# Decode stage of a two-layer hybrid trunk: one common step list replaced by a list for each engine

## The chip, the cores and the metric

The kernel runs on one core of a Trainium2 chip. The metric is device time in microseconds of one execution, the median of the runs. A core has TensorE (matrix products, here in fp32), VectorE, ScalarE, GpSimd and SyncE, which issues the DMAs; each works through its own instruction stream in order, and they wait for each other with counting semaphores.

## The reference, cut to what matters

One inference step through two layers. Each layer projects the input once and feeds three groups; the stage that is changed computes two of them side by side: the cached attention of eight decode rows, and the state recurrence of the 1024-token prompt.

```python
def mla_decode_attention(q_nope, q_pe, ckv, kpe, w_uk, w_uv, ckv_pool, kpe_pool, page_table):
    ckv_past = ckv_pool[page_table].reshape(B, -1, KV_LORA)      # 8 x 4096 x 256
    kpe_past = kpe_pool[page_table].reshape(B, -1, MLA_ROPE)     # 8 x 4096 x 64
    q_abs = jnp.einsum('blhd,rhd->blhr', q_nope, w_uk)
    s_past = (einsum(q_abs, ckv_past) + einsum(q_pe, kpe_past)) * ATTN_SCALE
    ...
    p = softmax(concatenate([s_past, s_new]))
    o_lat = einsum(p[..., :P], ckv_past) + einsum(p[..., P:], ckv)
    return einsum('blhr,rhd->blhd', o_lat, w_uv)

def rwkv7_time_mix(...):
    def step(S, inp):
        r_t, k_t, v_t, kk_t, b_t, d_t = inp
        sa = einsum('bhvk,bhk->bhv', S, kk_t)
        S = S * d_t[:, :, None, :] - sa[..., None] * b_t[:, :, None, :] + v_t[..., None] * k_t[:, :, None, :]
        return S, einsum('bhvk,bhk->bhv', S, r_t)
```

## The kernel before, in words

A layer is a sequence of blocks: the modulation, the projections with the prompt's attention, the decode stage, and the output projection. All engines meet between blocks. The decode stage (lines 1404 to 1860) does two things in one stream.

**Decode attention.** The 256 pages of a layer's cache are handled in 16 halves h of 16 pages (128 tokens each), two halves per decode row. SyncE fetches a half with two calls of `load` (lines 399 to 404), a quad q of eight pages of 160 KB each, page numbers read from the page table. The quads lie in a ring of six (QS = 6), so of three halves. For q from 6 on SyncE first waits for `pg_free`, which TensorE raises when PV has read the quad that lay there:

```python
for q in range(4, 2 * NH):
    if q >= QS:
        sp.wait_ge(pg_free, q - QS + 1)
    load(sp, q)
```

Ahead of quad 4 the same queue issues a few small transfers for the sample rows' state, and behind quad 5 eight small ones. Quads 0 to 3 are loaded before or at the start of the stage.

The steps of a half, with their lines:
- turn (L1748, VectorE): transposes one block of 32 rows in 128 x 512 elements, ten per half, n = 10 h + rb, into a ring of four buffers. The first of a half (rb = 0) waits for both quads (`pg_in`); each waits until TensorE has used the block four before it.
- S (L1589, TensorE): scores of one turned block, 16 matmuls in the trace per S (8 in the program). Ten per half.
- MX (L1808 to L1815, VectorE): the maximum; EX (L1690, ScalarE): the exponentials.
- PT (L1598, TensorE; L1700, ScalarE): transposes the probabilities.
- PV (L1607, TensorE): probabilities times pages, 32 matmuls in the trace; half-way and at its end it raises `pg_free`.

**State recurrence.** The prompt is handled in 8 pairs p of two chunks of 64 tokens; one pair goes with two halves, 2p and 2p+1. `prepare(p, n)` builds a pair's matrices: MA (L1467; VectorE L1764 to L1773, `levels` L1756), five levels of an inverse in which X (L1515; last L1494) goes from TensorE to a copy on ScalarE (L1664) and Y (L1522; last L1501, L1503) from TensorE to VectorE (L1781, L1783), then AK (L1474, L1777), TA and TB (L1480, L1482, L1487; ScalarE L1649, L1656). `follow(p, n)` carries the state through the pair before: Z (L1538, L1541; ScalarE L1670), U (L1549; L1674), H (L1556, L1558; VectorE L1791, then the scaled state `Sg`, L1795), OO (L1565 to L1569; L1677).

**What sets the order.** One list `plan` is walked by TensorE, VectorE and ScalarE alike; each does its part of a step or nothing. Per half it runs S S | two steps | S S | PT | two steps | S S | PV | two steps | S S | two steps | S S | step | MX | step | EX | step. PT and PV are those of the half before. Where the list says S of block n, VectorE makes the turn of block n + 2. After the last pair a tail does the last PT, PV, the last chain and the combination FC.

Of the kernel before, what the change touches and what calls it, by code (L numbers as in the profile page):

```python
# [26 lines left out]
S = 1024  # L27
NS = 8
T = S + NS
# [70 lines left out]
def bass_hybrid_trunk(nc, a):  # L100
    with ExitStack() as ctx:
# [92 lines left out]
        with nc.Fori(0, DEPTH) as layer:  # L194
# [345 lines left out]
            with nc.Block() as block:  # L540
# [517 lines left out]
                def _(dve):  # L1058
# [229 lines left out]
                    for what, n, x in plan:  # L1288
# [114 lines left out]

            STEPS = ["MA", "Z0", "X1", "U0", "Y1", "H0", "X2", "Z1", "Y2", "U1", "X3", "H1", "Y3", "OO",
                     "X4", "AK", "Y4", "TA", "X5", "TB", "Y5"]
            chain = ("Z", "U", "H", "O")


            plan = []
            for h in range(NH):  # L1410
                mine = [("rw", n) for n in (STEPS[0:11] if h % 2 == 0 else STEPS[11:])]
                for rb in range(0, NB, 2):
                    plan += [(h, "S", rb), (h, "S", rb + 1)]
                    if rb == 2 and h:
                        plan.append((h - 1, "PT", 0))
                    if rb == 4 and h:
                        plan.append((h - 1, "PV", 0))
                    if rb < 8:
                        plan += [(h // 2, *mine.pop(0)), (h // 2, *mine.pop(0))]
                rest = [(h // 2, *x) for x in mine]  # L1420
                plan += rest[:1] + [(h, "MX", 0)] + rest[1:2] + [(h, "EX", 0)] + rest[2:]
            plan += [(NH - 1, "PT", 0), (NS, "rw", "Z0"), (NH - 1, "PV", 0), (0, "FC", 1), (NS, "rw", "U0"), (0, "FC", 2), (NS, "rw", "H0"),
                     (0, "FC", 3), (NS, "rw", "Z1"), (0, "FC", 4), (NS, "rw", "U1"), (0, "FC", 5), (NS, "rw", "H1"), (0, "FC", 6),
                     (NS, "rw", "OO")]

            with nc.Block() as block:
# [25 lines left out]
                def _(pe):  # L1452
# [119 lines left out]

                    for h, what, g in plan:
                        if what == "rw" and g[0] in chain:
# [58 lines left out]
                def _(act):  # L1633
# [44 lines left out]

                    for h, what, g in plan:
                        if what == "rw" and g[0] in chain:  # L1680
# [57 lines left out]
                def _(dve):  # L1738
# [20 lines left out]
                    def prepare(p, n):  # L1759
                        k = p % 2  # L1760
                        B = PB[:, 5, :].rearrange("p (v d c) -> p v d c", v=2, d=4)
                        if n == "MA":
# [9 lines left out]
                            dve.drain()  # L1772
                            dve.transpose(Tm.rearrange("p d c -> p (d c)"), Tc.rearrange("p d c -> p (d c)")).then_inc(tm_done, 1)  # L1773
                            levels(2, LEVELS).then_inc(bm_done, 1)
                        elif n == "AK":
# [9 lines left out]
                    def follow(p, n):  # L1785
                        B = PB[:, 6, 0:P].rearrange("p (f v) -> p f v", f=2)
                        if n[0] == "H":
                            i = 2 * p + int(n[1])
                            dve.wait_ge(hh_full, i + 1)
                            for f in range(2):  # L1790
                                op = dve.scalar_tensor_tensor(S0[:, (i + 1) % 4, f, :], B[:, f, :], ecol[:, f, i:i + 1], Sg[:, f, :], ALU.mult, ALU.add)  # L1791
                            op.then_inc(st_done, 1)
                            if i + 1 < NCH:
                                dve.drain()
                                dve.tensor_tensor(Sg, S0[:, (i + 1) % 4], ecol[:, :, i + 1:i + 2].broadcast_to([P, 2, 64]), ALU.mult)  # L1795

                    for h, what, g in plan:
                        if what == "rw" and g[0] in chain:
                            if h >= 1:
                                follow(h - 1, g)  # L1800
                        elif what == "rw":
                            prepare(h, g)
                        elif what == "S":
                            if NB * h + g + 2 < NB * NH:
                                turn(NB * h + g + 2)
                        elif what == "MX":
# [377 lines left out]
```

## Time and profile before

| | us |
|---|---|
| median of 3 runs | 2041.21 |
| lowest and highest | 2038.88, 2041.49 |
| the profiled execution: its time | 2037.07 |
| the profiled execution: its span | 2035.4 |
| decode stage, layer 0 | 625 to 880 |
| decode stage, layer 1 | 1635 to 1893 |
| TensorE, VectorE, ScalarE busy | 1865.2, 895.6, 494.7 |

All times below are microseconds from the start of the profiled span. An engine's busy time leaves out semaphore waits and the issue of DMAs; a matmul's end is modelled. Waits are put down to the instruction that ended them. SPq is SyncE's DMA issue: a row "x16" there is 16 fetches issued one behind the other.

### The profile page before, as it was taken

The numbers are of one execution on the slowest core, as the hardware profiler recorded it, in microseconds if no ns is written. First come the engines' busy times: TensorE is split into PE (matmuls) and PEld (weight loads), VectorE is DVE, ScalarE is ACT, GpSimd is POOL, SyncE is SP. The second block draws the span as 40 slices with busy tenths as digits, with TensorE's granted clock in tenths as the row PEclk, the third lists the DMA queues.
The fourth block names the chain that finished last, engine by engine and source line by source line (L and its number), as shares of the span: only waits on it lengthen the run. The fifth ranks groups of instructions, "written<-read, shape, count | busy, mean of one in ns | idle before, by whom it ended". The sixth has DMA issues, their size and how long they took to land. (4 is left out here: it accounts for less than half of the span.)

```text
span 2035.4 us, 45818 instructions
## 1 busy us (share of the span) xinstructions
PE 1865.2 (92%) x19360; PEld 1164.3 (57%) x19360; DVE 895.6 (44%) x1984; ACT 494.7 (24%) x1164; POOL 172.6 (8%) x158
## 2 busy tenths in 40 slices
PE   4899999999987999899949999999999879998898
PEld 2565676666654666654326656766666546665543
DVE  2024134222766676654230340332318577775542
ACT  3111012222412333311131110222224123333201
POOL 0010000011334000000000100000212240000000
PEclk9899999999999999979989999999999899999899
DMA  9500000000205666341075001010001166562411
GB/s 388 207 11 27 21 21 32 21 21 13 59 26 159 185 188 180 109 178 42 32 301 213 0 27 32 11 32 22 21 22 50 28 186 186 176 186 83 178 42 42
DMA packets 103927, 191.18 MB, mean 94 GB/s; under 512 B 17162, under 2 KB 87260, under 8 KB 100004
## 3 DMA queue, kind: packets, MB, share of 16 engines
q1 hardware_dynamic: 103716, 188.19, 27.9%
q8 instruction: 154, 2.52, 0.5%
q14 instruction: 57, 0.47, 0.1%
HBM read 175.41 MB, written 21.19 MB: 97 GB/s over the span
## 5 line engine op out<-in xcount | busy, mean ns | idle before, releaser
L771 PE MATMUL PB<-RB,R 128*128 128x344 f32 x1632 | 496.1, 457 | 0.0
L771 PEld LDWEIGHTS PB<-RB,R 128*128 128x128 f32 x1632 | 303.7, 191 | 159.6 <-issue 19.7
L1946 PE MATMUL PB<-RB,R 128*128 128x512 f32 x512 | 221.2, 593 | 0.0
L1589 PE MATMUL PB<-WUQ,Q 32*32 32x256 f32 x5120 | 191.0, 385 | 14.7 <-DVE WUQ L1748 9.4
L1748 DVE STREAM_TRANSPOSE WUQ<-RB 128x512 f32<-128x512 f32 x316 | 197.0, 676 | 5.5 <-DMA RB<-in_cache 5.3
L1946 PEld LDWEIGHTS PB<-RB,R 128*128 128x128 f32 x512 | 97.0, 190 | 120.8 <-issue 118.6
L931 ACT ACTIVATE R<-PB 128x344 f32<-128x344 f32 x90 | 41.2, 457 | 423.4 <-PE PB L771 423.4
L1184 DVE TENSOR_TENSOR PB<-PB,CST 128x128 f32<-128x128 f32 x64 | 18.8, 294 | 226.3 <-PE PB L791 226.3
L1589 PEld LDWEIGHTS PB<-WUQ,Q 32*32 32x32 f32 x5120 | 90.0, 104 | 46.0 <-DVE WUQ L1748 23.1
L619 PE MATMUL PB<-RB,R 128*128 128x344 f32 x288 | 88.5, 472 | 10.8 <-PEq L225 10.8
L619 PEld LDWEIGHTS PB<-RB,R 128*128 128x128 f32 x288 | 57.1, 199 | 41.4 <-issue 14.8
L246 PE MATMUL PB<-R,WUQ 128*32 128x512 f32 x192 | 33.5, 667 | 49.2 <-DMA R<-in_w_ada 49.2
L1066 DVE COPY R<-PB 128x320 f32<-128x320 f32 x16 | 7.9, 491 | 149.7 <-PE PB L630 149.7
L788 PE MATMUL PB<-RB 128*128 128x128 f32 (+2 forms) x192 | 71.5, 495 | 0.0
L630 PE MATMUL PB<-RB 128*128 128x320 f32 x256 | 69.2, 432 | 0.0
L1607 PE MATMUL PB<-RB 128*32 128x256 f32 x1024 | 67.4, 404 | 1.9 <-ACT RB L1700 1.9
L2041 POOL TENSOR_TENSOR sm<-sm,small 128x1 f32<-128x1 f32 (+1 forms) x18 | 9.9, 550 | 698.6 <-DVE sm L2073 698.6
L942 ACT ACTIVATE R<-PB,sm,small 128x128 f32<-128x128 f32 (+3 forms) x64 | 53.2, 832 | 56.8 <-DVE sm L1188 56.2
L760 PE MATMUL PB<-R,RB 128*128 128x256 f32 x256 | 61.1, 383 | 0.0
L630 PEld LDWEIGHTS PB<-RB 128*128 128x128 f32 x256 | 48.6, 190 | 20.3
L1700 ACT ACTIVATE RB<-PB 64x256 f32<-64x256 f32 x128 | 48.3, 378 | 39.1 <-PE PB L1598 37.8
L2015 ACT ACTIVATE RB<-PB 128x1024 f32<-128x1024 f32 x16 | 16.3, 1021 | 161.2 <-PE PB L1946 161.2
(355 smaller groups left out, 2619.6 us busy)
## 6 DMA issues: line engine op xcount, KB each, us to landing
RB<-in_cache SPq DMA_DIRECT2D x512, 160.0 KB, 2.6
R<-in_w_ada SPq DMA_DIRECT2D x16, 1536.0 KB, 17.4
R<-in_w_in SPq DMA_DIRECT2D x44, 512.0 KB, 3.7
RB<-in_w_out SPq DMA_DIRECT2D x8, 1024.0 KB, 9.9
RB<-out_x_stream SPq DMA_DIRECT2D x2, 4096.0 KB
out_x_stream<-RB SPq DMA_DIRECT2D x16, 512.0 KB
RB<-in_x_prompt SPq DMA_DIRECT2D x1, 4096.0 KB
RB<-in_w_kv SPq DMA_DIRECT2D x2, 1280.0 KB, 5.6
```

The lines of the kernel that those rows point to most:

```text
L619: mm = pe.matmul(bigbank(n)[:, c, :], ring[:, i % 4, k, :], hT[:, k, c * CH:(c + 1) * CH], start=(k == 0), stop=(k == KT - 1))
L630: mm = pe.matmul(smlbank("kv", t)[:, 0:KVW], hT[:, k, cols(t)], wkv_in[:, k, :], start=(k == 0), stop=(k == KT - 1))
L760: mm = pe.matmul(jobbank(j)[:, 0:256].rearrange("p (w c) -> p w c", w=2), hT[:, k, cols(c)], w2, start=(k == 0), stop=(k == KT - 1))
L771: mm = pe.matmul(jobbank(j)[:, 0:CH], ring[:, blkno[n] % 4, k, :], hT[:, k, chunk(c)], start=(k == 0), stop=(k == KT - 1))
L788: pe.matmul(sbank(2 * u + e)[:, c:c + w], qT[:, h, i * P:(i + 1) * P], kT[:, h, c:c + w], start=True, stop=False)
L931: act.activation(to, jobbank(j)[:, 0:CH], fn).then_inc(pj_free[j % 2], 1)
L942: act.activation(pbuf(n), sbank(n), ACT.Exp, bias=nbr[:, n:n + 1], scale=scq[:, i:i + 1], accum_out=Lr[:, n:n + 1]).then_inc(ex_done, 1)
L1589: mm = pe.matmul(PB[qp[o], 2 * (h % 2) + q % 2, 0:256], Q4[qp[q], g, :], k[qp[q], c], start=(g == 0), stop=(g == NB - 1), skip_group_check ...
L1607: mm = pe.matmul(PB[qp[c], 7, f * KVL:(f + 1) * KVL], PT[:, s, 32 * c:32 * c + 32], qpage(q)[:, (4 * s + c) % 8, RP:RP + KVL], start=(h == ...
L1700: op = act.activation(PT[hp[w], :, e * 64:(e + 1) * 64], t4[hp[e], :, w, :], ACT.Identity)
L1748: op = dve.transpose(KTr[:, n % 4], pages[:, :, fcol(rb):fcol(rb) + 32])
L1946: mm = pe.matmul(PB[0:n, 2 * (t % 2) + hf, :], mixT[:, k, cols(t)], wo[:, k, hf * 512:(hf + 1) * 512], start=(k == 0), stop=(k == 5))
```

## The change

The common list `plan` goes. TensorE, VectorE and ScalarE get a list each for one pair, in words; `pair_plan` writes it out for p = 0 to 7 and appends the same tail. In a word, S or T and two digits are score or turn: the half of the pair and the block (T20 and T21 are the first two turns of the next pair). PT, PV, MX and EX carry 0 or 1 for the pair's halves, and - for the second half of the pair before. So turns stand singly in VectorE's list, and no longer two ahead of the same S.

Two steps are cut off from others on VectorE. LV is `levels(2, LEVELS)`, which was the end of MA. G is the scaled state `Sg`, which followed H at once, behind a drain; now it has its own place, and drains only in the tail. The computation, the buffers, the semaphores' meanings, SyncE's queue and GpSimd's work stay as they are.

```diff
-            plan = []
-            for h in range(NH):
-                mine = [("rw", n) for n in (STEPS[0:11] if h % 2 == 0 else STEPS[11:])]
...
+            PE_PAIR = (
+                "S00 Z0 MA S01 S02 S03 U0 S04 PT- H0 X1 S05 Y1 Z1 S06 U1 X2 S07 H1 S08 S09 S10 Y2 PV- X3 OO Y3 S11 AK "
+                "S12 X4 PT0 S13 TA Y4 S14 S15 S16 S17 S18 TB S19 X5 PV0 Y5"
+            ).split()
+            DVE_PAIR = (
+                "T02 T03 T04 MA T05 H0 T06 LV Y1 G0 T07 T08 T09 T10 T11 T12 Y2 H1 T13 MX0 G1 Y3 T14 AK T15 T16 T17 "
+                "T18 T19 Y4 T20 T21 MX1"
+            ).split()
+            ACT_PAIR = (
+                "Z0 U0 MA X1 Z1 U1 X2 PT- X3 OO EX0 X4 PT0 TA TB X5 Y5 EX1"
+            ).split()
...
+                        elif n == "LV":
                             levels(2, LEVELS).then_inc(bm_done, 1)
...
                             op.then_inc(st_done, 1)
+                        elif n[0] == "G":
+                            i = 2 * p + int(n[1])
                             if i + 1 < NCH:
-                                dve.drain()
+                                if p == NS - 1:
+                                    dve.drain()
                                 dve.tensor_tensor(Sg, S0[:, (i + 1) % 4], ecol[:, :, i + 1:i + 2].broadcast_to([P, 2, 64]), ALU.mult)
+                                if p == NS - 1:
+                                    dve.drain()
...
-                        elif what == "S":
-                            if NB * h + g + 2 < NB * NH:
-                                turn(NB * h + g + 2)
+                        elif what == "T":
+                            turn(NB * h + g)
```

**TensorE, where a PV stands.** Before, in the first half of pair 1, from the second S pair to PV (L1607). L1589 is S (x16 in the order is two S), L1598 PT, L1515 an X, L1549 U, L1522 a Y.

```order
L1589 MATMUL PB<-WUQ,Q 32x256 x16
L1598 MATMUL PB<-CST,grow 128x128 x4
L1515 MATMUL PB<-RB 32x32 x16
L1549 MATMUL PB<-RB,R 64x64 x4
L1589 MATMUL PB<-WUQ,Q 32x256 x16
L1607 MATMUL PB<-RB 32x256 x16
L1522 MATMUL PB<-RB 32x32 x16
```

Now, in the same pair: from U1 (L1557) and X2 (L1523) to the first PV (L1615). L1597 is S (x8 is one), L1564 and L1566 are H1, L1530 is Y2.

```order
L1557 MATMUL PB<-RB,R 64x64 x4
L1523 MATMUL PB<-RB 32x32 x16
L1597 MATMUL PB<-WUQ,Q 32x256 x8
L1564 MATMUL PB<-R 64x64 x2
L1566 MATMUL PB<-WUQ,R 64x64 x2
L1564 MATMUL PB<-R 64x64 x2
L1566 MATMUL PB<-WUQ,R 64x64 x2
L1597 MATMUL PB<-WUQ,Q 32x256 x24
L1530 MATMUL PB<-RB 32x32 x16
L1615 MATMUL PB<-RB 32x256 x16
```

PV of the half before stood behind the sixth S of its half's successor; now PV- stands behind the eleventh S of the pair, and the chain's H0, Z1, U1 and H1 are ahead of it.

**TensorE, the other PV of a pair.** Before, in the second half: X4, two S, PV, AK (L1474).

```order
L1515 MATMUL PB<-RB 32x32 x16
L1589 MATMUL PB<-WUQ,Q 32x256 x16
L1607 MATMUL PB<-RB 32x256 x16
L1474 MATMUL PB<-RB,R 64x128 x8
L1522 MATMUL PB<-RB 32x32 x16
```

Now, at the end of the pair: Y4, five S, TB (L1495), S19, X5 (L1502), PV0.

```order
L1530 MATMUL PB<-RB 32x32 x16
L1597 MATMUL PB<-WUQ,Q 32x256 x40
L1495 MATMUL PB<-CST,R 128x128 x2
L1597 MATMUL PB<-WUQ,Q 32x256 x8
L1502 MATMUL PB<-RB 32x32 x8
L1615 MATMUL PB<-RB 32x256 x16
```

It moved from behind the pair's sixteenth S to behind its twentieth, and AK, TA and TB now stand ahead of it.

**VectorE, the turns in the second half's beginning.** Before, from MX (L1808) through two turns (L1748), H1 with its scaled state (L1791, L1795) and Y3 to four turns.

```order
L1815 TENSOR_SCALAR sm<-sm,CST 128x1
L1748 STREAM_TRANSPOSE WUQ<-RB 128x512 x2
L1791 SCALAR_TENSOR_TENSOR R<-PB,ecol,RB 128x64 x2
L1795 TENSOR_TENSOR RB<-R,ecol 128x128
L1781 TENSOR_TENSOR RB<-RB,PB 128x128
L1783 STREAM_TRANSPOSE RB<-RB 128x128
L1748 STREAM_TRANSPOSE WUQ<-RB 128x512 x4
```

Now, from G0 (L1807) through the turns T07 to T12 (L1756), Y2 and H1 (L1800) to T13 and MX0.

```order
L1807 TENSOR_TENSOR RB<-R,ecol 128x128
L1756 STREAM_TRANSPOSE WUQ<-RB 128x512 x6
L1790 TENSOR_TENSOR RB<-RB,PB 128x128
L1792 STREAM_TRANSPOSE RB<-RB 128x128
L1800 SCALAR_TENSOR_TENSOR R<-PB,ecol,RB 128x64 x2
L1756 STREAM_TRANSPOSE WUQ<-RB 128x512
L1821 TENSOR_REDUCE sm<-PB 128x1
```

T10, the first turn of the second half and the one that waits for that half's pages, now stands fourth in a row of six turns, ahead of Y2, H1 and MX0.

## Rows read from the trace of the kernel before

**Rows 1.** The page: busy us (share of the span) x instructions, by engine.
```profile
PE 1865.2 (92%) x19360; PEld 1164.3 (57%) x19360; DVE 895.6 (44%) x1984; ACT 494.7 (24%) x1164; POOL 172.6 (8%) x158
```
**Rows 2.** Windows, pairs 2 to 6: us, PE, PEld, DVE, ACT, POOL busy, PEclk, DMA, GB/s.
```profile
684.55:831.50 146.95, 135.37 (x4334) 91.97 (x4325) 105.95 (x261) 54.11 (x171) 0.00 (x0) 1.00 0.61 182
1696.30:1843.80 147.50, 136.15 (x4336) 92.06 (x4326) 105.94 (x261) 54.12 (x171) 0.00 (x0) 1.00 0.61 182
```
**Rows 3.** TensorE's waits, 686 to 833: waiter <- releaser: total us, times, longest.
```profile
PE PB L1467 <- ACT R L1661: 2.2, 5, 0.4
...
PE PB L1515 <- DVE RB L1773: 2.0, 5, 0.4
...
PE PB L1589 <- DVE WUQ L1748: 1.1, 5, 0.2
```
**Rows 4.** SyncE's fetches: timeline (start, us, xcount); issue to landing; waits, 680 to 880.
```profile
653.12 10.92 SPq L404 DMA_DIRECT2D RB<-in_cache  x16
...
664.95 10.76 SPq L404 DMA_DIRECT2D RB<-in_cache  x16
...
679.29 10.39 SPq L404 DMA_DIRECT2D RB<-in_cache  x16
...
723.20 12.59 SPq L404 DMA_DIRECT2D RB<-in_cache  x16
...
752.16 12.02 SPq L404 DMA_DIRECT2D RB<-in_cache  x16
...
1663.41 10.52 SPq L404 DMA_DIRECT2D RB<-in_cache  x16
...
1675.38 11.95 SPq L404 DMA_DIRECT2D RB<-in_cache  x16
...
1838.52 11.71 SPq L404 DMA_DIRECT2D RB<-in_cache  x16
...
DMA to landing us min/median/max: 2.0/2.6/4.1
...
SPq L401 <- PE PB L1607: 25.0, 10, 3.5
```
**Rows 5.** Timeline: first turn and score of pair 1, and the tail's PT.
```profile
650.46 1.30 DVE L1748 STREAM_TRANSPOSE WUQ<-RB 128x512 f32<-128x512 f32 x2 [2.20 <-DMA RB<-in_cache]
...
651.32 0.45 PE L1589 MATMUL PB<-WUQ,Q 32*32 32x256 f32 x8 [1.17 <-DVE WUQ L1748]
...
862.96 0.66 PE L1598 MATMUL PB<-CST,grow 128*128 128x128 f32 x4 [2.08 <-ACT grow L1690]
```
**Rows 6.** Timeline of pair 4, layer 0, from S00; TensorE, then VectorE's maximum.
```profile
742.81 0.37 PE L1589 MATMUL PB<-WUQ,Q 32*32 32x256 f32 x1
...
750.26 1.93 PE L1607 MATMUL PB<-RB 128*32 128x256 f32 x32
752.12 0.45 PE L1522 MATMUL PB<-RB 32*32 32x32 f32 x32
...
757.30 0.45 PE L1515 MATMUL PB<-RB 32*32 32x32 f32 x32 [0.42 <-DVE RB L1783]
...
767.79 1.15 PE L1589 MATMUL PB<-WUQ,Q 32*32 32x256 f32 x32
768.87 0.44 PE L1480 MATMUL PB<-CST,RB 128*128 128x128 f32 x2
...
771.77 0.37 PE L1589 MATMUL PB<-WUQ,Q 32*32 32x256 f32 x1
...
757.17 0.65 DVE L1808 TENSOR_REDUCE sm<-PB 128x1 f32<-128x512 f32 x1
...
758.65 1.29 DVE L1748 STREAM_TRANSPOSE WUQ<-RB 128x512 f32<-128x512 f32 x2
```
**Rows 7.** Windows around a lower granted clock (PEclk), layer 1; columns as in rows 2.
```profile
1659.50:1670.90 11.40, 5.50 (x163) 3.31 (x148) 9.49 (x18) 5.02 (x17) 10.84 (x6) 1.00 0.51 147
1670.90:1674.30 3.40, 3.37 (x48) 1.41 (x52) 1.75 (x3) 0.00 (x0) 1.22 (x4) 0.51 0.77 238
```

More of the change, by code:

```diff
@@ L1402, in bass_hybrid_trunk @@
             fcol = lambda rb: RP + 32 * rb if rb < 8 else 32 * (rb - 8)
-            STEPS = ["MA", "Z0", "X1", "U0", "Y1", "H0", "X2", "Z1", "Y2", "U1", "X3", "H1", "Y3", "OO",
-                     "X4", "AK", "Y4", "TA", "X5", "TB", "Y5"]
-            chain = ("Z", "U", "H", "O")
-            plan = []
-            for h in range(NH):
-                mine = [("rw", n) for n in (STEPS[0:11] if h % 2 == 0 else STEPS[11:])]
[L1412 to L1421, printed above, removed]
@@ L1422, in bass_hybrid_trunk @@
-            plan += [(NH - 1, "PT", 0), (NS, "rw", "Z0"), (NH - 1, "PV", 0), (0, "FC", 1), (NS, "rw", "U0"), (0, "FC", 2), (NS, "rw", "H0"),
-                     (0, "FC", 3), (NS, "rw", "Z1"), (0, "FC", 4), (NS, "rw", "U1"), (0, "FC", 5), (NS, "rw", "H1"), (0, "FC", 6),
-                     (NS, "rw", "OO")]
+            chain = ("Z", "U", "H", "G", "O")
+            PE_PAIR = (
+                "S00 Z0 MA S01 S02 S03 U0 S04 PT- H0 X1 S05 Y1 Z1 S06 U1 X2 S07 H1 S08 S09 S10 Y2 PV- X3 OO Y3 S11 AK "
+                "S12 X4 PT0 S13 TA Y4 S14 S15 S16 S17 S18 TB S19 X5 PV0 Y5"
+            ).split()
@@ new lines, in bass_hybrid_trunk, with pair_plan @@
+            DVE_PAIR = (
[5 more added lines that the diff above has]
+            ).split()
+            def pair_plan(words):
+                out = []
+                for p in range(NS):
+                    for w in words:
+                        if w[0] in "ST" and w[1] in "012":
+                            out.append((2 * p + int(w[1]), w[0], int(w[2])))
+                        elif w[:2] in ("PT", "PV", "MX", "EX"):
+                            out.append((2 * p - 1 if w[2] == "-" else 2 * p + int(w[2]), w[:2], 0))
+                        else:
+                            out.append((p, "rw", w))
+                return [x for x in out if 0 <= x[0] < NH] + TAIL
@@ L1426, in bass_hybrid_trunk @@
+            TAIL = [(NH - 1, "PT", 0), (NS, "rw", "Z0"), (NH - 1, "PV", 0), (0, "FC", 1), (NS, "rw", "U0"), (0, "FC", 2), (NS, "rw", "H0"),
+                    (NS, "rw", "G0"), (0, "FC", 3), (NS, "rw", "Z1"), (0, "FC", 4), (NS, "rw", "U1"), (0, "FC", 5), (NS, "rw", "H1"),
+                    (0, "FC", 6), (NS, "rw", "OO")]
             with nc.Block() as block:
@@ L1571, in follow @@
                             mm.then_inc(oo_full, 1)
-                    for h, what, g in plan:
+                    for h, what, g in pair_plan(PE_PAIR):
                         if what == "rw" and g[0] in chain:
@@ L1677, in follow @@
                             act.activation(A3[:, :, p * P:(p + 1) * P], PB[:, 6, 0:2 * P].rearrange("p (f t) -> p f t", f=2), ACT.Identity).then_inc(oo_done, 1)
-                    for h, what, g in plan:
+                    for h, what, g in pair_plan(ACT_PAIR):
                         if what == "rw" and g[0] in chain:
@@ L1792, in follow @@
                             op.then_inc(st_done, 1)
+                        elif n[0] == "G":
+                            i = 2 * p + int(n[1])
                             if i + 1 < NCH:
-                                dve.drain()
+                                if p == NS - 1:
+                                    dve.drain()
                                 dve.tensor_tensor(Sg, S0[:, (i + 1) % 4], ecol[:, :, i + 1:i + 2].broadcast_to([P, 2, 64]), ALU.mult)
-                    for h, what, g in plan:
+                                if p == NS - 1:
+                                    dve.drain()
+                    for h, what, g in pair_plan(DVE_PAIR):
                         if what == "rw" and g[0] in chain:
```

## The prediction, made before the result

> **What bounds the kernel now.** Read the page first: TensorE is busy for 92% of the span, VectorE for 44% [rows 1]. So only what moves TensorE's work, or the waits in it, can move the end. The change touches one stage, the decode stage, which runs once in each of two layers (625 to 880 us and 1635 to 1893 us). Its eight pairs p = 0 to 7 repeat one pattern; I call the start of a pair's first score step S00, and of the first step of its second half S10.
>
> Second, the windows over pairs 2 to 6 [rows 2]: 146.95 and 147.5 us for five pairs, so **a pair takes 29.4 and 29.5 us**, of which TensorE is busy 27.1 and 27.2 and VectorE 21.2. Third, TensorE's waits in that stretch [rows 3]: many of 0.2 to 0.7 us each, on VectorE and ScalarE in turn; with the smaller rows of that answer they make 2.3 us per pair. These are the waits that own lists can take away. Were they all to go, the pair would take 27.1 us. VectorE, at 21.2 us busy, could follow.
>
> Fourth, and this decides my forecast, the queue that fetches the pages. A half needs 16 pages; they go into a ring of three halves, and SyncE may fetch those of half h only when the PV step of half h-3 has read the old ones. In that queue a half's 16 fetches take 10.4 to 12.6 us [rows 4]; the 22 halves from the one at 679.29 to the one at 1838.52 that were fetched apart have a mean of 11.3. Landing comes 2.6 us (median) after a fetch's issue. Today SyncE still waits for PV, 25.0 us in ten halves of layer 0 [rows 4], so the queue has some 2.5 us to spare per half, and VectorE waits for pages only once per layer, at pair 1, by 2.2 us in layer 0 [rows 5].
>
> **The way from a PV to the scores that need its ring place.** Step by step: PV starts at 750.26, the first fetch at 752.16 [rows 4, 6]: 1.9 us. 16 fetches: 11.3. Last issue's end to landing: 2.6 less its own 0.33, 2.27. Turning the first block, to the score on it: 650.46 to 651.32 [rows 5], 0.86. Sum **16.3 us** (15.4 to 17.6 with the shortest and longest fetches). Today PV starts 7.45 us after S00 (742.81 to 750.26) and the S00 that needs its pages comes at 771.77, 21.5 us after that PV [rows 6]: 5 us of slack.
>
> **The change part by part.**
>
> *PV moves back.* In the new TensorE list PV- stands behind eleven S steps instead of six, and behind H0, Y1, Z1, U1, X2, H1 and Y2 as well. The cost in front of it: 7.45, less the 1.1 us of waits in it (2.2, 2.0 and 1.1 us in five pairs, ahead of MA, X1 and the third pair of S [rows 3]), plus five S at 0.54 (32 matmuls, two S, are started in 1.08, 767.79 to 768.87) 2.7, plus Y1 to U1 without their four S, 752.12 to 756.88, 4.76 - 2.16 = 2.6, plus H1, which I put at 0.8, twice the mean of those six steps [rows 6]: 12.4 us after S00. PV0 comes at the pair's end, behind S19 and X5. With a pair of 27.1 us the first leaves 14.7 us until the next S00, and PV0 (two S, Y2, and what follows up to X5: about 12.8 us after S10) leaves 27.1 - 12.8 = 14.3 until the next S10. Both are under 16.3. **So the waits on VectorE and ScalarE go, and a wait for pages takes their place.**
>
> The new period follows from two loops. First: S00, 12.4 us to PV-, 16.3 to the next S00; I add 0.5 because VectorE, which stood at T20, has then two turns of 0.6, the maximum (1.5) and T02 to T04 to do, which makes S03, S05 and S07 some 0.2 us late each [rows 6]. Sum 29.2. Second, since SyncE fetches in order: S10, 1.0 us to PV-, 1.9 to the first fetch, both halves' fetches 23.3 (10.92 + 10.76, and 10.52 + 11.95, back to back, with what lies between [rows 4]), and 3.1 to the score: 29.3. Both say **29.2 us per pair**, against 29.4 and 29.5: 5 x 0.2 + 5 x 0.3 = 2.5 us gained in both layers. Bounds: fetches of 10.4 or 12.6 in every half give 28.3 and 30.5; means over ten halves will lie closer, 28.5 to 29.9, or -7 to +7 us in all against the 29.2.
>
> *Start of the stage.* Pair 1 starts when quads 4 and 5 have landed, at 651.32 in layer 0 [rows 5]; layer 1 has the same wait. Their fetches stand behind small transfers, not behind a PV, so what pair 0 gains is lost again: nothing. Pair 1's S10 needs the next half, whose fetches end at 664.04 and 1673.93 whatever TensorE does [rows 4]: S10 at 667.2 and 1677.1. PV- is 1.0 later, the first fetch 1.9, the last issue 11.3, the score 3.1: S00 of pair 2 at 684.5 and 1694.4, against 684.55 and 1696.3, where the windows of [rows 2] begin: 0 and 1.9 us gained.
>
> *End of the stage.* Pair 7 fetches nothing. From its S10, 12.0 us after S00, remains 27.1 - 11.4 = 15.7 us of work, then ScalarE's Y5 and the last exponentials, of which 1.3 us stand alone: the tail's PT starts 29.0 us after S00 instead of 31.46 (831.50 to 862.96) [rows 2, 5]. Gained 2 x 2.5 = 5.0.
>
> *The rest.* LV behind a turn and G apart from H put 0.44 and 0.2 us of VectorE behind other work; X2, which needs LV, comes some 1 us after it, and only the tail keeps its waits for drains. A drain less per chunk is idle time on VectorE. More changes between shapes on TensorE could cost too, but S is followed by a step on all rows eight times a pair, before and after. All of this lies beside the wait for pages, with 2 us of cover per pair: 0.
>
> **Sum**: 2.5 + 1.9 + 5.0 = 9.4 us. The profiled execution took 2037.07 (span 2035.4), 4.1 less than the median 2041.21: it would become 2027.7, and the median **2031.8 us**.
>
> **A page against the rows.** Fetches of 160 KB bring 182 GB/s over a pair [rows 2], and back to back no half came under 10.5 us [rows 4]. The Trainium skill (DMA: Bandwidth & Descriptors, section Bandwidth) gives 341 GB/s for a transfer of 1 MB; by that figure a half of 2.6 MB would be moved in an estimated 7.7 us. It would make the first rival below come true; the trace does not agree with it, since SyncE issued without a wait for PV at 653 to 676 us and was no faster.
>
> **The rivals.**
>
> *TensorE stays the bound.* If fetches get by with 9 us a half, or the queue can run ahead as I don't see it, pairs take 27.1 us: 5 x 2.3 + 5 x 2.4 = 23.5 gained, with start and end 1.9 to 14 and 5.0: 1999 to 2011 us. For it: each single wait in [rows 3] does go. Against it: [rows 4], no half is that short. Chance 0.12.
>
> *The clock falls in the new wait: slower.* I trade many short waits for one of some 2 us ahead of each S00. Between 1659.5 and 1670.9 TensorE was busy for 5.50 us of 11.4, and in the 3.4 us behind it the granted clock was 0.51, the lower of its two levels (1.2 of 2.4 GHz), [rows 7], against 1.00 over the ten periods of [rows 2]. If that happens in each of the ten periods, up to 1.7 us is lost between S00 and PV-, right in the first loop: 29.2 + 1.6 = 30.8 per pair, 16 us more: 2048 us. It decides from about 0.5 us per pair on. Against it: the new wait stands alone among dense work. Chance 0.12.
>
> *The gain at start and end is there, but a pair costs 29.7 or more* (longer fetches, as the 12.59 in [rows 4], or a landing of over 3 us under load): 2035.5 to 2041, within the same. Chance 0.12.
>
> **How the numbers follow.** Forecast with pairs of 28.3 to 29.7 us: 0.64, 2022 to 2036 us. Faster by over 0.2% (below 2037.1; about what a measurement can tell from no change): 0.64 + 0.12 and a little of the third case, 0.78. Within 0.2%: 0.12. Slower: 0.10, the clock's case less its mild forms. For 8 in 10, the range reaches into both neighbours: 2011 to 2042 us.
>
> **What would show it.** After the change VectorE waits for in_cache pages some 12 times per layer, at T20 by about 2 us, at T10 by less; SyncE hardly waits for PV any more; PV- starts 12 to 13 us behind S00; the pair takes 29.2 us; TensorE's waits on X1, X2, MA and TA are gone, and one on the page turn has come. The first rival shows pairs of 27 us and no wait for pages. The second shows a granted clock below 1 in the windows of pairs 2 to 6. I am wrong if a half's fetches take under 10 us when four quads follow each other.

## The result, and the profile after

The changed kernel is **slower**: 2049.58 us median of 6 runs (2047.45 to 2057.08), beside 2039.89 us (2037.92 to 2041.49) for the kernel before in the same comparison. The ratio is 1.0052, with a 95% interval of 1.0036 to 1.0069. The forecast was 2031.8 us, in a range of 2011 to 2042: wrong in sign, and the time lies outside the range. The profiled execution took 2051.55 us (span 2049.9), 14.5 more than that of before.

Lines of the change moved by eight: S is now L1597, PV L1615, the turn L1756, MA L1475. The page first: TensorE is busy for 12 us more than in [rows 1], with the same number of instructions.

```profile
PE 1877.4 (92%) x19360; PEld 1173.4 (57%) x19360; DVE 898.1 (44%) x1984; ACT 494.5 (24%) x1164; POOL 172.1 (8%) x158
```

Then the windows over pairs 2 to 6, the columns as in [rows 2]. The pairs take 31.7 and 31.0 us where they took 29.4 and 29.5, and the granted clock is no longer 1.00.

```profile
687.00:845.50 158.50, 143.70 (x4318) 96.11 (x4323) 107.61 (x261) 53.81 (x170) 0.00 (x0) 0.95 0.57 170
1705.80:1861.00 155.20, 140.42 (x4312) 93.23 (x4313) 106.83 (x261) 54.20 (x170) 0.00 (x0) 0.98 0.58 173
```

The waits from 684 to 835 us (waiter, releaser, total, times, longest). Of TensorE's waits of [rows 3], those on MA and X are gone. The one on the turn (L1589 there, L1597 here) has grown from 1.1 to 12.6 us, and ahead of it VectorE waits for pages (in_cache).

```profile
DVE WUQ L1756 <- DMA RB<-in_cache: 26.3, 7, 5.4
...
PE PB L1597 <- DVE WUQ L1756: 12.6, 6, 3.1
```

From 1690 to 1850 us the same two lines read 23.1 and 11.2:

```profile
DVE WUQ L1756 <- DMA RB<-in_cache: 23.1, 6, 5.1
...
PE PB L1597 <- DVE WUQ L1756: 11.2, 7, 2.7
```

VectorE waited at the first turn of every pair (T20, 2.9 to 5.4 us in the ten pairs 2 to 6), and at T10 in four of the ten. SyncE's own waits for PV from 680 to 885 us grew from 25.0 [rows 4] to 39.9. One sign of the prediction said that SyncE would hardly wait for PV any more; it waits longer, because PV- is late:

```profile
SPq L401 <- PE PB L1615: 39.9, 9, 8.7
```

One passage shows the whole mechanism: the timeline from S10 (764.45) and PV- (765.36) of pair 4 to the start of pair 5, layer 0 (start, us, line, xcount, and in brackets the idle time ahead and who ended it).

```profile
764.45 0.67 PE L1597 MATMUL PB<-WUQ,Q 32*32 32x256 f32 x16 [1.60 <-DVE WUQ L1756]
...
765.36 1.93 PE L1615 MATMUL PB<-RB 128*32 128x256 f32 x32
...
782.16 1.30 DVE L1756 STREAM_TRANSPOSE WUQ<-RB 128x512 f32<-128x512 f32 x2 [5.09 <-DMA RB<-in_cache]
...
783.02 0.67 PE L1597 MATMUL PB<-WUQ,Q 32*32 32x256 f32 x16 [1.98 <-DVE WUQ L1756]
...
784.48 1.92 PE L1475 MATMUL PB<-RB 64*64 64x128 f32 x16
```

PV- starts at 765.36; the pages that its end lets in are turned at 782.16; VectorE had waited 5.09 us for them, and TensorE starts S00 at 783.02 after 1.98 us of nothing. Between PV- and S00 lie 17.7 us. Behind that wait MA takes 1.92 us for 16 matmuls. Before it took 1.09:

```profile
744.44 1.09 PE L1467 MATMUL PB<-RB 64*64 64x128 f32 x16 [0.45 <-ACT R L1661]
```

The reason stands in a window laid over it: in the 3.4 us from 783.80 on, the granted clock is 0.51, the lower of the two levels.

```profile
783.80:787.20 3.40, 3.40 (x56) 2.68 (x62) 3.09 (x10) 0.95 (x3) 0.00 (x0) 0.51 0.77 220
718.90:725.70 6.80, 5.55 (x88) 3.61 (x96) 5.81 (x14) 0.95 (x3) 0.00 (x0) 0.50 0.77 227
```

Such stretches begin at 688.1, 718.9 (6.8 us long), 783.7, 814.4 and 845.1 in layer 0 and at 1705.3 and 1780.4 within the pairs of layer 1, all within 2 us of an S00, but for the last, which lies at an S10. In the ten pairs 2 to 6 that makes six; the one at 845.1 belongs to pair 7. Before there was none in them.

### The profile page after: what moved, and what is told of

Read it like the earlier page. It is cut to its first block and busy times, and to the rows that moved or that the text cites. A ratio compares the mean times of both kernels' runs of the same rounds, so it can differ in the third digit from the quotient of the medians.

```text
span 2049.9 us, 45792 instructions
## 1 busy us (share of the span) xinstructions
PE 1877.4 (92%) x19360; PEld 1173.4 (57%) x19360; DVE 898.1 (44%) x1984; ACT 494.5 (24%) x1164; POOL 172.1 (8%) x158
## 3 DMA queue, kind: packets, MB, share of 16 engines
q1 hardware_dynamic: 103716, 188.19, 27.8%
## 5 line engine op out<-in xcount | busy, mean ns | idle before, releaser
L1756 DVE STREAM_TRANSPOSE WUQ<-RB 128x512 f32<-128x512 f32 x316 | 205.6, 686 | 100.7 <-DMA RB<-in_cache 75.7
L1597 PE MATMUL PB<-WUQ,Q 32*32 32x256 f32 x5120 | 200.5, 395 | 44.8 <-DVE WUQ L1756 37.8
L1597 PEld LDWEIGHTS PB<-WUQ,Q 32*32 32x32 f32 x5120 | 85.3, 106 | 85.5 <-issue 60.1
L619 PE MATMUL PB<-RB,R 128*128 128x344 f32 x288 | 89.0, 474 | 10.8 <-PEq L225 10.8
L1615 PE MATMUL PB<-RB 128*32 128x256 f32 x1024 | 63.6, 387 | 2.5 <-ACT RB L1708 2.1
L1672 ACT ACTIVATE RB<-PB 128x128 f32<-128x128 f32 x80 | 22.2, 278 | 137.5 <-PE PB L1523 135.4
## 6 DMA issues: line engine op xcount, KB each, us to landing
R<-in_w_ada SPq DMA_DIRECT2D x16, 1536.0 KB, 17.1
```

Source lines behind the costliest of these rows:

```text
L619: mm = pe.matmul(bigbank(n)[:, c, :], ring[:, i % 4, k, :], hT[:, k, c * CH:(c + 1) * CH], start=(k == 0), stop=(k == KT - 1))
L1597: mm = pe.matmul(PB[qp[o], 2 * (h % 2) + q % 2, 0:256], Q4[qp[q], g, :], k[qp[q], c], start=(g == 0), stop=(g == NB - 1), skip_group_check ...
L1615: mm = pe.matmul(PB[qp[c], 7, f * KVL:(f + 1) * KVL], PT[:, s, 32 * c:32 * c + 32], qpage(q)[:, (4 * s + c) % 8, RP:RP + KVL], start=(h == ...
L1756: op = dve.transpose(KTr[:, n % 4], pages[:, :, fcol(rb):fcol(rb) + 32])
```

## The experiments

All whole times are medians, of the number of executions given, or one single execution where it says so. "Pairs" are means over pairs 2 to 6, layer 0 / layer 1. For comparison: before 29.39 / 29.50, after 31.69 / 31.05.

### Half of the pages fetched, in both kernels

Every second page is left out of the fetch (the rest is computed on what lies there), so SyncE's queue has half the work and the same semaphores.

```diff
-                for j, r in enumerate(regs):
+                for j, r in enumerate(regs[0:8:2]):
...
-                                dve.wait_ge(pg_in[q % QS], 128 * (q // QS + 1))
+                                dve.wait_ge(pg_in[q % QS], 64 * (q // QS + 1))
```

> The changed kernel, but only every second page is fetched (8 fetches per half in place of 16; the other places keep what lay there, so the decode attention is computed on wrong data). Ring theory: the way from PV to scores falls from 17.3 to some 11.5 us, nothing waits for pages any more, a pair takes 27 to 27.8 us, the whole about 2010 us. List theory: the pair stays at 31 us, since the lists, not the pages, set it. Clock theory: as ring theory if the wait goes.

> The kernel before, with the same cut: only every second page is fetched (decode attention on wrong data). Control for the run above. Ring theory: before the change the way of the pages had 5 us of slack, so only pair 1's wait changes: pairs 2 to 6 stay at 29.0 to 29.5 us, the whole at 2025 to 2037 us. If pairs get shorter by more than 0.5 us, the fetches cost TensorE or VectorE something by their traffic, in both kernels.

Measured, single executions: the changed kernel takes 1994.13 us, with pairs of 27.12 / 27.72; the kernel before 2029.98 us, with 29.20 / 29.67. The window 680 to 810 us of the changed kernel:

```profile
680.00:810.00 130.00, 128.82 (x4156) 88.22 (x4156) 103.06 (x250) 51.47 (x164) 0.00 (x0) 1.00 0.35 100
```

TensorE is busy for 128.82 of 130 us, there is no wait for pages, and the clock stays at 1.00. This settles the larger question. Without the wait the own lists do what the prediction's "TensorE stays the bound" said of them: 27.12 and 27.72 us a pair, and 36 us less in the whole than the common list under the same condition (20 of them in the ten pairs 2 to 6, most of the others at the start and the end of the two stages). With all pages that is lost again: 2049.6 less 1994.1 is 55 us. The same cut is worth 10 us to the kernel before (2030 against 2040). It halves the bytes, the fetches and their packets together; the next run parts the bytes from the other two.

### The same bytes halved another way: half of the columns

All pages are fetched, but only the first half of each row; the number of fetches is unchanged.

```diff
-                    sp.dma_start(qpage(q)[:, j], a["cache"][lay, bass.ds(page, 1), :, 0:KW].rearrange("l o p c -> (l o p) c")).then_inc(pg_in[q % QS], 16)
+                    sp.dma_start(qpage(q)[:, j, 0:KW // 2], a["cache"][lay, bass.ds(page, 1), :, 0:KW // 2].rearrange("l o p c -> (l o p) c")).then_inc(pg_in[q % QS], 16)
```

> The changed kernel; every page is still fetched with its own DMA, but only its first 160 of 320 columns (80 KB instead of 160; the other columns keep what lay there, so the decode attention is computed on wrong data). It parts the queue's issue time from the bytes. If a half's 16 fetches cost their issue alone (0.57 us each and 0.6 per quad, 10.0 us together) and land 2.2 us later, the way is 1.9 + 10.0 + 1.9 + 0.9 = 14.7, with 13 us from S00 to PV- the pair takes 27.7 to 28.5 us: bytes were worth some 3 us a pair, the whole about 2010 to 2018 us. If bytes play no part, the fetches stay at 11 to 12 us, the landing at 3 us and the pair at 31. If only the landing shortens, about 30.

Measured: 2039.32 us in one execution, pairs 30.66 / 30.25. The window 680 to 840 us:

```profile
680.00:840.00 160.00, 145.19 (x4406) 99.53 (x4406) 112.56 (x274) 54.82 (x174) 0.00 (x0) 0.95 0.34 91
```

91 GB/s instead of 170, and still 16 fetches take 11.1 to 12.6 us in the halves that S00 needs. What shortened is the end: from the last issue to the turn 1.6 to 3.3 us (mostly 1.7) instead of 1.9 to 3.8. So of the three outcomes expected the last came nearest, and the price of 10.0 us for a half's issues was too low (11.7 on average). The time of a half in the queue does not go with the bytes. It goes with the number of fetches, 5.8 us for eight in the run above, or with the number of their packets: a fetch is some 140 packets in either run, so these two are not parted. That is why half of the pages helped by 55 us and half of the columns by 10.

### The wait filled with work: is it the clock?

Two matmuls of 512 columns into an unused bank stand ahead of each pair's S00, where TensorE would wait for the pages anyway.

```diff
+                            if g == 0 and h >= 2 and h % 2 == 0:
+                                for _ in range(2):
+                                    pe.matmul(PB[:, 4, :], ident, CST[:, 0:512], start=True, stop=True, skip_group_check=True)
```

> The changed kernel with two extra matmuls of the identity by 512 columns into PSUM bank 4, which nobody reads, in front of each pair's S00 (about 1.7 us of work in a wait of 2 to 3 us). Clock theory: the granted clock stays at 1.00 in pairs 2 to 6, S00 to PV- shrinks from 13.9 to about 12.9 us, a pair from 31.4 to about 30.4, the whole to about 2039 us. Ring theory without the clock: the pair stays at 31.2 to 31.6 us, since the work lies in a wait. If the filler is longer than the wait, pairs get slower by the difference.

Measured: 2043.0 us (10 executions; ratio to before 1.0021, interval 1.0004 to 1.0038), pairs 30.64 / 30.44. So a kernel with more work is 6.6 us faster than the changed one (the kernel before stood at 2039.9 beside both). The window of its pairs 2 to 6 and the two rows that show the filler (L1595) and S00 (L1601) behind it:

```profile
684.40:837.60 153.20, 145.81 (x4330) 94.19 (x4329) 106.79 (x260) 53.50 (x169) 0.00 (x0) 1.00 0.60 175
```

```profile
776.11 1.98 PE L1595 MATMUL PB<-CST 128*128 128x512 f32 x4
778.02 0.66 PE L1601 MATMUL PB<-WUQ,Q 32*32 32x256 f32 x16
```

The clock is at 1.00 throughout; no lower stretch is left in pairs 2 to 6 of either layer. The filler is sometimes longer than the wait: here the turn behind the wait started at 776.50, and S00, which elsewhere follows it by 0.77 to 0.86 us, only at 778.02, when the filler was through. VectorE's wait for pages is the same:

```profile
DVE WUQ L1760 <- DMA RB<-in_cache: 26.4, 7, 5.5
```

So, as far as the filler itself takes nothing, the falls of the clock cost 1.05 and 0.61 us per pair, and what remains above the kernel before, about 1.1 us per pair, is the page loop by itself.

### The place of PV alone, in the kernel before

The common list stays; PV goes back from behind the sixth S of a half to behind the tenth, once ahead of what follows there, once behind it.

```diff
-                    if rb == 4 and h:
-                        plan.append((h - 1, "PV", 0))
...
+                if h:
+                    plan.append((h - 1, "PV", 0))
```

> The kernel before, with its common list, each PV moved from behind the sixth S of its half to behind the tenth. Ring theory: PV then starts some 11.7 us behind the half's first S, which leaves 29.4 - 11.7 = 17.7 us to the scores that need its place, against a way of 17.3: hardly a change, pairs of 29.4 to 30.0, the whole 2037 to 2047 us. If a later PV costs by itself (order on TensorE), the same loss would come here as in the next run.

> The kernel before, with its common list, each PV moved to the end of its half, just ahead of the next half's first S. Ring theory: PV starts some 13.7 us behind the half's first S, and 13.7 + 17.3 = 31.0 us come round for two halves: pairs of 31 us or a little more, with waits for pages on VectorE in every half, the whole 2052 to 2062 us. If it stays at 2040 to 2045 us, the place of PV in the list does not matter and the ring theory falls.

Measured, single executions: with the nearer place 2044.57 us, pairs 29.95 / 30.36, PV 11.4 to 12.5 us behind S00 (7.45 before). With the farther place 2075.56 us, pairs 33.15 / 33.44, PV- 13.7 to 16.8 us behind S00, and lower clocks in seven of the ten pairs. In both the wait for pages appears (684 to 835 us), the nearer place first, and in the second TensorE's wait at an X, whose Y stands behind the waiting turn in VectorE's list:

```profile
DVE WUQ L1748 <- DMA RB<-in_cache: 20.4, 10, 3.4
```

```profile
DVE WUQ L1748 <- DMA RB<-in_cache: 25.2, 8, 4.8
...
PE PB L1515 <- DVE RB L1783: 10.6, 5, 4.1
```

A late PV is enough to make the old list slower too, by 0.6 to 0.9 us a pair at the nearer place and by 3.8 to 3.9 at the farther; nothing else of the change is needed for it. The nearer place came out about as expected, though its 2044.57 us alone says little (the kernel before ran from 2035.93 to 2044.36 beside it). The farther one came 13.6 us above the range expected of it: that had PV 13.7 us behind the half's first S, and held neither the wait at X nor the lower clock.

### PV earlier in the new lists

Four kernels keep the own lists and bring PV forward (with ScalarE's PT- ahead of it); the last two move a few other steps as well. First, PV- alone to behind S05 (the first line below, with PV0 left where it was), and both, PV- behind S05 and PV0 behind S14:

```diff
-                "S00 Z0 MA S01 S02 S03 U0 S04 PT- H0 X1 S05 Y1 Z1 S06 U1 X2 S07 H1 S08 S09 S10 Y2 PV- X3 OO Y3 S11 AK "
-                "S12 X4 PT0 S13 TA Y4 S14 S15 S16 S17 S18 TB S19 X5 PV0 Y5"
+                "S00 Z0 MA S01 S02 S03 U0 S04 PT- H0 X1 S05 PV- Y1 Z1 S06 U1 X2 S07 H1 S08 S09 S10 Y2 X3 OO Y3 S11 AK "
+                "S12 X4 PT0 S13 TA Y4 S14 PV0 S15 S16 S17 S18 TB S19 X5 Y5"
```

> Only PV- is brought forward (behind S05), PV0 stays behind X5. Ring theory: the loop over S00 goes, the one over PV0 stays: PV0 some 13 us behind S10, 17.3 us to the next S10, so a pair takes 29.8 to 30.8 us, with the wait for pages at T10 and none at T20. If the late PV0 costs nothing, the pair is as with both early, 30.2 us or less without a wait for pages.

> The changed kernel with its two PV steps brought forward: PV- from behind Y2 to behind S05 (ScalarE's PT- from behind X2 to behind MA), PV0 from behind X5 to behind S14. Ring theory (the way from a late PV to the scores that need its place in the ring sets the pair): PV- then starts some 7 us behind S00, the way of 17.3 us fits into a pair, the waits for pages go, and a pair takes 27 to 27.8 us against 31.4 now: about 2005 to 2015 us. Clock theory (the falls of TensorE's clock cost the time, the wait alone would not): falls vanish only if the wait does, so the same time is expected, but with the wait left and full clock a pair of about 30. List theory (the own lists, with single turns, cost time by themselves on TensorE and VectorE): pairs stay above 29.4 us and waits on the page turn stay, now on TensorE's use of the ring of four blocks.

PV- alone: 2041.14 us in one execution, pairs 30.02 / 30.49. PV0 stayed 12.6 to 14.6 us behind S10, and what is left of the wait for pages (684 to 835 us) is mostly the other half's, at T10:

```profile
DVE WUQ L1756 <- DMA RB<-in_cache: 6.8, 5, 3.7
```

Both: 2034.0 us (10 executions; ratio 0.9967, interval 0.9954 to 0.9980), faster than before, and no wait for pages is left in pairs 2 to 6. The 2005 to 2015 us and the pairs of 27 to 27.8 us that were expected of it did not come: the pairs of its profiled execution (2039.24 us, its slowest) take 30.12 / 30.34. That is what they take with PV- alone, so the loss of that kernel can't be put down to its late PV0 by this pair of runs. Waits on the inverse's chain came back (TensorE, 684 to 835 us), since X3 now follows Y2, and Y5 (L1509) follows X5, with no PV between them:

```profile
PE PB L1523 <- DVE RB L1792: 4.0, 5, 0.8
PE PB L1509 <- ACT RB L1672: 3.4, 5, 0.7
...
PE PB L1530 <- issue: 2.0, 3, 1.3
```

So the next list spreads the chain's steps as well (Y2 ahead of S09 and S10, S18 and S19 between TB, X5 and Y5; VectorE's H1 ahead of Y2 and T12):

```diff
+                "S00 Z0 MA S01 S02 S03 U0 S04 PT- H0 X1 S05 PV- Y1 Z1 S06 U1 X2 S07 H1 S08 Y2 S09 S10 X3 OO Y3 S11 AK "
+                "S12 X4 PT0 S13 TA Y4 S14 PV0 S15 S16 S17 TB S18 X5 S19 Y5"
```

> PV- and PV0 early as in the run before, and the places mended where TensorE still waited there: Y2 stands behind S08 and ahead of S09 and S10 (it was right ahead of X3, which waited 0.8 us for VectorE), TB behind S17, and S19 between X5 and Y5 (Y5 waited 0.7 us for ScalarE); VectorE does H1 and Y2 ahead of T12. Ring theory with waits between engines added: the 1.4 us of these waits per pair go, a pair takes 28.7 to 29.2 us instead of 30.2, the whole 2018 to 2026 us. If TensorE is instead held up by something the lists don't show (its idle time put down to issue, 0.4 to 1.5 us a time), the pair stays near 30 and the whole at 2030 us or above.

2027.0 us (6 executions, 2024.81 to 2030.05; ratio 0.9936, interval 0.9920 to 0.9951), pairs 29.78 / 29.01: faster than both kernels, and 1 us above the range that the ring theory gave. Now TensorE waits mostly for "issue", so for nothing that the profile names (681.4 to 830.2 us):

```profile
PE PB L1530 <- issue: 2.7, 2, 1.8
PE PB L1597 <- issue: 2.6, 3, 1.0
PE PB L1509 <- ACT RB L1672: 1.1, 5, 0.2
```

Is it the pages' traffic? The same kernel with half of the pages:

> The kernel with both PV early and the places mended, with every second page fetched only (decode attention on wrong data). It no longer waits for pages; what is left of its idle time on TensorE is put down to issue, 7 us in five pairs. Traffic theory: that idle time comes from the pages' traffic (TensorE's own code comes in through the same 16 DMA engines), so it goes with half of the pages, the pair falls from 29.4 to 27.2 us, the whole to about 2000 us. List theory: the idle time comes from the order and stays, pair 29 us, the whole 2020 us or above.

2017.84 us in one execution, pairs 28.75 / 28.50. Only some 9 us come from the pages; neither theory was right alone. The rest of the distance to 1994 belongs to the order itself: with the same half traffic this list takes 0.8 to 1.6 us more per pair than the changed one. The two differ in the places of Y2, TB, S19 and H1 too, so that is not the price of PV's place by itself.

Last, PV as late as the ring seems to allow: PV- behind H1 (after S07), which is 4 us later than in the list before, and PV0 behind S15, in time 9.4 us behind S10 (9.6 there). VectorE's H1 stands one turn earlier, ahead of T11, and ScalarE's PT- behind X1:

```diff
+                "S00 Z0 MA S01 S02 S03 U0 S04 PT- H0 X1 S05 Y1 Z1 S06 U1 X2 S07 H1 PV- S08 Y2 S09 S10 X3 OO Y3 S11 AK "
+                "S12 X4 PT0 S13 TA Y4 S14 S15 PV0 S16 S17 TB S18 X5 S19 Y5"
```

> After pv_early2 (2027.0 us, pairs of 29.78 and 29.01 us), with the two PV blocks moved to the latest place that the page ring seems to allow: PV- behind the seventh S step of the even half (S07), PV0 behind S15. Theory A, the loop over the page ring decides: from PV to the scores that need its ring place 17.3 us pass in the changed kernel (1.9 + 11.5 + 3.1 + 0.9), and PV- would end some 10.5 us after S00, so the loop is 27.8 us, under the 29 us of pv_early2; what is left is TensorE's own work, near 27.1 us a pair, and its small waits on the other engines, which get more time to deliver because the score steps stand closer together ahead of PV. Pairs of 28.0 to 29.0, whole 2005 to 2022 us, hardly any wait of VectorE for in_cache. Theory B, TensorE's idle time without a named releaser (some 7 us in 150 in pv_early2) belongs to the dense small score matmuls and not to the place of PV: pairs stay at 29.0 to 29.8, whole 2024 to 2032. Theory C, PV any later than in pv_early2 is already too late for the ring (landings of 3 to 4 us under traffic): VectorE's page turn waits for in_cache again by over 2 us in several pairs, TensorE waits behind it and its clock falls; 2035 or more.

**2018.8 us** (5 executions, 2016.08 to 2022.2; before, beside it, 2036.39; ratio 0.9906, interval 0.9891 to 0.9921), pairs 28.54 / 28.94. Time and pairs are those of theory A. Its windows over pairs 2 to 6:

```profile
680.80:823.40 142.60, 137.57 (x4324) 89.05 (x4315) 107.90 (x262) 54.11 (x170) 0.00 (x0) 1.00 0.63 188
1685.00:1829.70 144.70, 138.71 (x4342) 89.22 (x4328) 107.26 (x261) 54.17 (x170) 0.00 (x0) 1.00 0.62 185
```

PV- starts 10.8 and 11.1 us behind S00. With the measured way of 17.3 us (below) the ring allows 28.1 and 28.4 us per pair, and the pair is barely above it. The wait for pages is not gone, as theory A would have it: VectorE shows it in both layers, in layer 1 in the way of theory C (680.8 to 823.4 us, then 1680 to 1850 us). But it seldom reaches TensorE, which waits for the turn not at all in pairs 2 to 6 of layer 0 and once, for 0.7 us, in those of layer 1:

```profile
DVE WUQ L1756 <- DMA RB<-in_cache: 6.9, 5, 2.4
...
DVE WUQ L1756 <- DMA RB<-in_cache: 18.2, 10, 3.6
```

### G joined with H again

Does the separate scaled state matter? In the list with PV behind S05, G goes back behind H with a drain.

```diff
-                "T02 T03 T04 MA T05 H0 T06 LV Y1 G0 T07 T08 T09 T10 T11 H1 Y2 T12 T13 MX0 G1 Y3 T14 AK T15 T16 T17 "
+                "T02 T03 T04 MA T05 H0 G0 T06 LV Y1 T07 T08 T09 T10 T11 H1 G1 Y2 T12 T13 MX0 Y3 T14 AK T15 T16 T17 "
...
-                                if p == NS - 1:
-                                    dve.drain()
+                                dve.drain()
```

> The kernel with both PV early and the places mended, but the scaled state again at once behind H with its drain, as before the change (the tail as changed). It measures that part of the change alone. Expected: VectorE has room here (21.5 of 29.4 us busy), so 0 to +2 us against 2027.0. If the scaled state's own place mattered, the drain would hold T06 and T12 back by 0.3 us each, 0.6 us a pair, +8 us or more.

2027.93 us (6 executions; ratio 0.9947, interval 0.9927 to 0.9967) beside 2027.0 (0.9936, interval 0.9920 to 0.9951): no difference that can be told.

## Why the prediction was wrong, point by point

**What held.** TensorE's short waits went. The wait for pages took their place, at S00 by way of VectorE's T20. TensorE's own work in a pair is near 27.1 us: the run with half of the pages shows pairs of 27.12 and 27.72. G's own place is worth nothing that can be told, as costed (tried in the list with both PV early; LV's was not tried alone). The sum's structure was right too: PV's place plus the way through the ring is the pair.

**The step that failed: the first loop, "12.9 + 16.3 = 29.2".** Measured over pairs 2 to 6 of both layers (means of ten):

| from | to | predicted | after | with the filler |
|---|---|---|---|---|
| S00 | PV- | 12.9 | 14.1 | 13.4 |
| PV | first fetch | 1.9 | 2.0 | |
| 16 fetches | last issue's end | 11.3 | 11.4 | |
| last issue's end | turn | 2.27 | 3.0 | |
| turn | S00 | 0.86 | 0.86 | |
| way through the ring | | 16.3 | 17.3 | 17.1 |
| pair | | 29.2 | 31.4 | 30.5 |

*The landing: 0.7 us too small.* I took the median of all landings, 2.6 us. But the turn waits for all 16 pages, so what counts is the last landing. Most of this stood in the trace of before and needed no run. Here are its last fetches at 835.1 and 836.7 and its last four up to 1833.3 (landing min/median/max):

```profile
DMA to landing us min/median/max: 2.5/3.0/3.5
```

```profile
DMA to landing us min/median/max: 2.6/2.7/4.1
```

Over the halves h = 4 to 15 of both layers, the slowest of the last four fetches lands 3.4 us after its own issue on average before (2.5 to 4.1). It is not always the one issued last: from the end of the last issue to the last landing it takes 2.6 us on average (1.9 to 3.8), and a turn that waits starts 0.12 us behind the last landing. That makes 2.8 instead of my 2.27. After, in the halves that S00 needs, it is 3.0; the slowest lands after 3.5 us there, as in the last four up to 715.3 us:

```profile
DMA to landing us min/median/max: 2.5/2.7/3.8
```

Put into the sum, 2.8 gives pairs of 29.7 instead of 29.2: in ten pairs 2.5 us lost instead of 2.5 gained, and at the start, where the term stands twice, 0.9 lost in layer 0 and 0.9 gained in layer 1 instead of 0 and 1.9. With the 5.0 of the end 2.5 us would be left of 9.4. With the 3.0 of after it would be 1 us lost. **Most of the gain that I forecast, if not all, was this one term.** My bound for the way, 15.4 to 17.6, moved only the fetch time and held the landing fixed.

*S00 to PV-: 1.2 us too small,* the larger part of the 2.2 us between 29.2 and 31.4. 0.7 of it goes when the filler stands in the wait, so most of that is the lower clock: MA at 1.92 for 1.09 us is the largest single piece. The other 0.5 stays with the clock at 1.00, and it is idle time, not work. With half of the pages S00 to PV- takes 12.5 us, about my 12.4 without the addition of 0.5. With the filler TensorE stands idle between S00 and PV- for 0.9 us per pair, 0.3 with half of the pages, and most of the difference is a wait at S10 for T10, so for the other half's pages (1.60 us at 764.45 in the rows above). The first loop held no such wait.

**Two rivals that I held apart came together.** The third, "a landing of over 3 us under load", and the second, the clock in the new wait, had 0.12 each as alternatives. They are not alternatives: a longer way makes a longer wait, at most of these waits the clock fell, and the slower work ahead of PV- lengthens the loop again. The second rival's price was 1.6 us per pair, if in each; the filler puts it at 1.05 and 0.61, since six such stretches fell into the ten pairs, not ten. That its 2048 us lies so near the measured 2049.58 is luck: the clock is less than half of what a pair lost against the forecast. My argument against it, "the new wait stands alone among dense work", was no protection: the lower clock followed a wait of 1.98 us at 783.02. One of 2.41 us at 1829.16 was not followed by it.

**The second loop** (SyncE in order, 29.3) used the same landing. It decided less often: T10 waited for pages in four of the ten pairs, T20 in all ten. It also leaves SyncE without work for 6 us a pair (29.3 less 23.3), which my sign "SyncE hardly waits for PV any more" contradicts; the measured 39.9 us fit the loop and not the sign.

**Start of the stage.** Predicted 0 and 1.9 us gained. From S00 of pair 0 to S00 of pair 2 layer 0 lost 2.2 and layer 1 gained 1.0: in layer 0 pairs 1 and 2 start at 653.1 and 687.0 us after against 651.3 and 684.6, with a lower clock from 654.0 on, a stretch that I had taken as unchanged.

**End of the stage.** Predicted 2.5 us each. From S00 of pair 7 to the tail's PV it takes 31.76 and 33.48 us, against 33.75 and 33.88: 2.0 and 0.4 gained. The wait in front of pair 7 was accompanied by a lower clock in both layers (from 845.1 and 1862.3).

**The sum**, as it came out: 0.2 us lost ahead of the stage, pairs 11.5 + 7.8 lost, start 2.2 lost and 1.0 gained, end 2.4 gained: 18.3 us. The profiled executions differ by 14.5. The other 3.8 came back behind the two stages' last PV (1.5 and 2.3). In layer 0 one 3.4 us stretch of lower clock fewer lies there; the rest was not taken apart. The medians differ by 9.7; the two profiled executions lie on opposite sides of their medians, by 2.0 and 2.8.

**The page against the rows.** I had kept SyncE's 11.3 us against the 7.7 us estimated by the Trainium skill (DMA: Bandwidth & Descriptors, section Bandwidth, 341 GB/s for 1 MB, measured there with transfers issued from GpSimd). The measurement decides for the row and shows in part why: with half of the bytes in as many fetches the time stays (11.7 against 11.4 us), so bytes were not what set it.

## What to carry to other kernels

A step that frees a ring place belongs into the sum as a loop: its own place, plus the whole way until the first reader, with the *last* landing of the group, not a median; here half a microsecond there was most of the forecast gain. A new wait of 2 to 3 us in front of dense matmuls can bring the lower clock with it, so price both together. And when the lists are free, try the latest place that the ring allows: with PV- 7, 10.9 and 14 us behind S00 the kernels took 0.9936, 0.9906 and 1.0052 of the time of before, each beside its own comparison, so the middle one is faster by some 6 and 30 us. The lists differ in a few other places too, so not all of it is PV's.

## What the runs showed of the hardware that I had not expected

- **Waits of 2 to 3 us were mostly accompanied by a lower clock.** From pair 2 to S00 of pair 7 TensorE waited ten times for 1.96 to 3.3 us for a turn, with the engine busy before. At eight of them the granted clock was 0.51 for 3.4 us (6.8 once), beginning between 1.3 us ahead of the wait's end and 1.4 us behind it. At two (1.96 us ahead of 1799.17 and 2.41 us ahead of 1829.16) it stayed at 1.00, so the length of the wait alone does not tell. Two dummy matmuls ahead of each S00 left no such stretch in the ten pairs and saved 6.6 us in the whole.
- **Halving the bytes of a fetch leaves its time in SyncE's queue.** 16 fetches take 10.1 to 12.5 us with 160 KB each and 11.1 to 12.6 us with 80 KB (halves that S00 needs, pairs 2 to 6). One takes 0.33 us at least and now and then more, with 0.52 us for each load of page numbers (SyncE, 690 to 850 us of the changed kernel: duration min/median/max in ns):

```profile
L404 SPq DMA_DIRECT2D RB<-in_cache x163: 332/333/1787, 689.5 to 849.4; - x163
```

```profile
L401 SPq TENSOR_LOAD <-lnb x20: 521/524/538, 703.1 to 847.5; - x20
```

- **Some orders leave TensorE idle with nobody to name, and these gaps go with packets of code.** Lists with PV behind S05 show "issue" gaps of up to 1.8 us and 6 to 7 us of them in five pairs (2027.0 us kernel); half of the pages leaves 4.6 us of them. With PV behind H1 they are 0.9 us at most and 3 us in five pairs. The traces tell what they go with. In pairs 2 to 6 of all fourteen there are 64 unnamed gaps of over 0.5 us, and each ends 1.2 to 1.6 us after the end of a packet of 16 KB on the queue for instructions (q8); a moment taken at random lies 1.1 to 1.7 us behind such an end in 14% of cases. For the gap of 1.76 us that ends at 784.70 (2027.0 us kernel) that packet runs from 782.28 to 783.34. The Trainium skill (Runtime: NRT & Kernel Launch, section Instruction fetch mechanics) says that code is fetched in blocks of 16 KB while the engine works and that this is mostly hidden; by these packets the gaps look like the part that isn't hidden. No run changed how the code comes in, so that it is the cause is argued from the times alone, and why some orders have more such gaps than others stays open.
